# Channel norms of a two-block layer kernel: square roots and reciprocals taken once per token instead of on full tiles

## The reference, cut to what matters

```python
# first block, RWKV branch: the key's unit length over each head of 64 channels
kk = kk / jnp.maximum(jnp.sqrt(jnp.sum(kk * kk, axis=-1, keepdims=True)), 1e-12)
# after the scan: group norm over each head of 64 channels, then gain, bias, bonus, gate
mu = jnp.mean(y, axis=-1, keepdims=True)
var = jnp.mean(jnp.square(y - mu), axis=-1, keepdims=True)
y = (y - mu) * lax.rsqrt(var + GN_EPS) * gn_g + gn_b
y = (y + jnp.sum(r * k * r_k, axis=-1, keepdims=True) * v) * jax.nn.silu(gate)
# latents of both blocks: rmsnorm over 256, 128, 384 and 256 channels, layernorm over 64
y = xf * lax.rsqrt(jnp.mean(xf * xf, axis=-1, keepdims=True) + eps) * g
# second block, twice: rmsnorm over each head of 128 channels, times a gate
o = _rmsnorm(o, out_norm) * jax.nn.silu(g_raw)
```

## Time and profile before

| | us |
|---|---|
| median of 3 runs (6708.9 to 6734.62) | 6714.53 |
| the profiled execution, its own time | 6711.7 |
| its span | 6710.1 |

### The profile page before, as it was taken

One profiled execution on the slowest core, in us unless ns is written; L12 is line 12 of the kernel. 1 busy time (PEld: TensorE's weight loads), 2 busy tenths in 40 slices (PEclk: granted clock), 3 DMA queues, 4 the chain that ended last, 5 costly groups with the idle time before them and its releaser, 6 DMA issues. The chain is left out here.

```text
span 6710.1 us, 96643 instructions
## 1 busy us (share of the span) xinstructions
PE 5494.9 (82%) x37796; PEld 4606.1 (69%) x37797; DVE 3000.2 (45%) x4371; ACT 2172.1 (32%) x3224; POOL 263.6 (4%) x318
## 2 busy tenths in 40 slices
PE   5954774869685878999896859769999999999994
PEld 3642762657562457999785625659898898898994
DVE  3696334441264234555413633334444455554544
ACT  2212112532221334444422213223333344444432
POOL 0120000000010000000000100010000000000000
PEclk8976997979897888999898978879999999999997
DMA  2110001022000035555310000454444455555544
GB/s 72 39 44 2 3 13 57 1 109 72 16 0 28 7 123 226 204 206 201 139 63 13 0 32 2 167 177 159 156 160 155 163 184 189 184 188 188 188 160 167
DMA packets 112191, 714.18 MB, mean 106 GB/s; under 512 B 12960, under 2 KB 16816, under 8 KB 70320
## 3 DMA queue, kind: packets, MB, share of 16 engines
q1 hardware_dynamic: 96208, 657.53, 27.1%
q0 software_dynamic: 9184, 28.49, 1.2%
q10 hardware_dynamic: 6528, 24.12, 0.9%
HBM read 639.42 MB, written 70.67 MB: 106 GB/s over the span
## 5 line engine op out<-in xcount | busy, mean ns | idle before, releaser
L2702 DVE TENSOR_TENSOR experts_low<-experts_raw,experts_high 128x1024 fp32r<-128x1024 f32 x678 | 810.8, 1224 | 1000.5 <-ACT experts_high L2631 1000.5
L2566 PE MATMUL ps<-experts_xs_high,experts_high 128*128 128x256 f32 (+1 forms) x3584 | 1040.4, 290 | 31.6 <-issue 29.8
L2566 PE MATMUL ps<-experts_xs_low,experts_high 128*128 128x256 f32 (+1 forms) x3584 | 1040.0, 290 | 6.7 <-issue 6.7
L2566 PE MATMUL ps<-experts_xs_high,experts_low 128*128 128x256 f32 (+1 forms) x3584 | 1041.5, 291 | 0.0
L2566 PEld LDWEIGHTS ps<-experts_xs_high,experts_high 128*128 128x128 f32 x3584 | 682.3, 190 | 44.2 <-issue 34.7
L2631 ACT ACTIVATE experts_high<-experts_raw 128x1024 fp32r<-128x1024 f32 x678 | 687.7, 1049 | 63.1 <-DMA experts_raw<-experts 63.1
L2566 PEld LDWEIGHTS ps<-experts_xs_low,experts_high 128*128 128x128 f32 x3584 | 682.4, 190 | 16.3 <-issue 7.3
L2566 PEld LDWEIGHTS ps<-experts_xs_high,experts_low 128*128 128x128 f32 x3584 | 682.4, 190 | 0.0
L2250 PE MATMUL ps<-dense_xs_parts,dense_high 128*128 128x256 f32 x2816 | 499.2, 280 | 3.9 <-DVE dense_xs_parts L2353 2.7
L2250 PEld LDWEIGHTS ps<-dense_xs_parts,dense_high 128*128 128x128 f32 x2816 | 437.0, 189 | 12.2 <-issue 4.7
L2558 PE MATMUL ps<-experts_high,experts_hid_high 128*128 128x512 f32 x1120 | 445.1, 397 | 0.0
(11 more groups left out here) (492 smaller groups left out, 9428.1 us busy)
## 6 DMA issues: line engine op xcount, KB each, us to landing
experts_raw<-experts SPq DMA_DIRECT2D x226, 1536.0 KB, 6.4
dense_raw<-dense SPq DMA_DIRECT2D x90, 1536.0 KB, 6.6
proj_raw<-w_in SPq DMA_DIRECT2D x41, 512.0 KB, 3.6
y_slot<-route_blank SPq DMA_DIRECT2D x15, 1152.0 KB, 20.8
out_proj_raw<-w_out SPq DMA_DIRECT2D x48, 256.0 KB, 2.6
proj_keys_raw<-w_in SPq DMA_DIRECT2D x20, 512.0 KB, 3.5
x_mixed<-x_out SPq DMA_DIRECT2D x16, 512.0 KB, 4.8
y_slot<-experts_y ACTq DMA_DIRECT2D x8, 1024.0 KB, 8.7
```

What stands on the lines that cost most here:

```text
L2566: last = nc.tensor.matmul(ps[:, m, 0:width], w[:, u, m, c], x[:, k, 0:width], start=(k == 0 and i == 0), stop=(k == KD - 1 and i == 2))
L2702: nc.vector.tensor_tensor(low[:, v, t, :], raw[:, v % NR, t, :], high[:, v, t, :].bitcast(F32), ALU.subtract).then_inc(split, 1)
```

## The change

In all seven stages the sums are now formed with tokens on partitions. A block of 128 channels by 128 tokens of squares is PE's stationary operand, and one or two columns of ones move through it: out comes one number for each token (and head), with tokens on partitions. A tile gives 8 columns (16 with two heads to a tile). On this small array `stat` (`length` in `operands`, where all four tiles make one array of 64 columns) DVE scales, ACT takes the root, DVE inverts. Then ACT copies each number along 128 (64) columns into the tile that held the squares ("spread"), PE transposes the eight 128x128 blocks of it into PSUM ("turned"), and DVE multiplies it in from there. In `rwkv_out`, DVE's steps are also merged: gain and inverse in one instruction, bias and bonus in another. The tiles' steps are interleaved instead of step by step over all tiles, except in `operands`.

`head_norm_gate`, the core of it (`channel_norms` has the same form, with `ones` and groups of tiles):

```diff
@@ head_norm_gate, scalar
                 act.wait_ge(meansq, j + 1)
-                nc.scalar.activation(sq[:, j, :], sq[:, j, :], ACT.Sqrt).then_inc(rooted, 1)
+                nc.scalar.activation(stat[:, 1, j, :], stat[:, 0, j, :], ACT.Sqrt).then_inc(rooted, 1)
+                act.wait_ge(inverse, j + 1)
+                nc.scalar.activation(spread[j], stat[:, 2, j, :].unsqueeze(2).to_broadcast([P, NT, P]), ACT.Copy).then_inc(spreaded, 1)
@@ head_norm_gate, tensor
+            def sum_tokens(j):
+                pe.wait_ge(squared, j + 1)
+                if j >= 2:
+                    pe.wait_ge(meansq, j - 1)
+                for b in range(NT):
+                    last = nc.tensor.matmul(core.ps[:, 6 + j % 2, b:b + 1], sq[:, j, b * P:(b + 1) * P],
+                                            core.c("ones")[:, 0:1], start=True, stop=True)
+                last.then_inc(sums, 1)
+
+            def turn(j):
+                pe.wait_ge(spreaded, j + 1)
+                if j >= 3:
+                    pe.wait_ge(normed, j - 2)
+                for b in range(NT):
+                    last = nc.tensor.transpose(two(j)[:, b * P:(b + 1) * P], spread[j][:, b, :], core.c("eye"))
+                last.then_inc(turned, 1)
             for j in range(4):
-                pe.wait_ge(squared, j + 1)
-                for h in range(2):
-                    last = nc.tensor.matmul(core.ps[:, 2 * j + h, :], core.c("ones"), sq[:, j, h * HALF:(h + 1) * HALF],
-                                            start=True, stop=True)
-                last.then_inc(sums, 1)
+                sum_tokens(j)
+                if j >= 1:
+                    turn(j - 1)
+            turn(3)
@@ head_norm_gate, vector
+            def apply(j):
+                dve.wait_ge(gated, j + 1)
+                dve.wait_ge(turned, j + 1)
+                nc.vector.scalar_tensor_tensor(dst[:, j, :], dst[:, j, :], gain, two(j), ALU.mult, ALU.mult).then_inc(normed, 1)
...
```

`rwkv_operands`:

```diff
@@ scalar
+            act.wait_ge(lengths, 1)
+            nc.scalar.activation(length[:, 0, :], core.ps[:, 0, 0:8 * NT], ACT.Sqrt).then_inc(rooted, 1)
+            act.wait_ge(inverse, 1)
             for j in range(4):
-                act.wait_ge(heads, j + 1)
-                nc.scalar.activation(tmp[:, j, :], two(j), ACT.Sqrt).then_inc(rooted, 1)
+                nc.scalar.activation(tmp[:, j, :].rearrange("p (b n) -> p b n", b=2 * NT),
+                                     length[:, 2, 2 * NT * j:2 * NT * (j + 1)].unsqueeze(2).to_broadcast([P, 2 * NT, 64]),
+                                     ACT.Copy).then_inc(spreaded, 1)
@@ vector
+            nc.vector.tensor_scalar(length[:, 1, :], length[:, 0, :], 1e-12, None, ALU.max).then_inc(bounded, 1)
+            dve.wait_ge(bounded, 1)
+            nc.vector.reciprocal(length[:, 2, :], length[:, 1, :]).then_inc(inverse, 1)
             for j in steps:
...
-                dve.wait_ge(inverse, j + 1)
-                nc.vector.tensor_tensor(KK[:, j, :], KK[:, j, :], tmp[:, j, :], ALU.mult).then_inc(unit, 1)
+                dve.wait_ge(turned, j + 1)
+                nc.vector.tensor_tensor(KK[:, j, :], KK[:, j, :], two(j), ALU.mult).then_inc(unit, 1)
```

`rwkv_output`, DVE's new order:

```diff
+            def scale(j):
+                dve.wait_ge(centred, j + 1)
+                dve.wait_ge(turned, j + 1)
+                nc.vector.scalar_tensor_tensor(dev[:, j, :], dev[:, j, :], core.v("gn_g", j), two(1 + j % 3), ALU.mult, ALU.mult)\
...
+            for j in range(6):
+                if j < 4:
+                    invert(j)
+                if 1 <= j < 5:
+                    scale(j - 1)
+                if j >= 2:
+                    add(j - 2)
+                    give(j - 2)
```

More of the change, by code:

```diff
@@ L964, in _, with sum_tokens, turn @@
         def _(pe):
+            def sum_tokens(i):
+                g = groups[i]
+                pe.wait_ge(squared, sum(len(y[0]) for y in groups[:i + 1]))
+                if i >= 2:
+                    pe.wait_ge(meansq, i - 1)
+                for b in range(NT):
+                    for m, c in enumerate(g[0]):
+                        last = nc.tensor.matmul(core.ps[:, i % 2, b:b + 1], sq[:, c, b * P:(b + 1) * P],
+                                                core.c("ones")[:, 0:1], start=(m == 0), stop=(m == len(g[0]) - 1))
+                last.then_inc(sums, 1)
+            def turn(i):
+                pe.wait_ge(spreaded, i + 1)
+                for b in range(NT):
+                    last = nc.tensor.transpose(two(2 + 2 * i)[:, b * P:(b + 1) * P], spread[i][:, b, :], core.c("eye"))
+                last.then_inc(turned, 1)
             for i, g in centred:
@@ L968, in _ @@
                 last.then_inc(mean_ready, 1)
-            done = 0
-            for i, g in enumerate(groups):
-                done += len(g[0])
-                pe.wait_ge(squared, done)
-                for h in range(2):
-                    for m, b in enumerate(g[0]):
-                        last = nc.tensor.matmul(core.ps[:, 2 * i + h, :], core.c("heads" if g[4] else "ones"),
-                                                halves(sq[:, b, :], h), start=(m == 0), stop=(m == len(g[0]) - 1))
-                last.then_inc(sums, 1)
+            for i in range(len(groups)):
+                sum_tokens(i)
+                if i >= 1:
+                    turn(i - 1)
+            turn(len(groups) - 1)
         @block.scalar
@@ L1008, in _ @@
                     nc.vector.tensor_scalar(x[:, g[0][0], :], x[:, g[0][0], :], core.v(g[4], 0), None, ALU.add)
+            for i in range(len(groups)):
+                invert(i)
+                if i >= 1:
+                    apply(i - 1)
+            apply(len(groups) - 1)
     st.end()
@@ L1892, in head_norm_gate @@
     sq = st.sb("sq", [P, 4, T])
-    two = lambda j: core.ps[:, 2 * j:2 * j + 2, :].rearrange("p b n -> p (b n)")
-    squared, sums, gated, meansq, rooted, inverse = (st.sem(x) for x in ("squared", "sums", "gated", "meansq", "rooted", "inverse"))
+    stat = st.sb("stat", [P, 3, 4, NT])
+    spread = [sq[:, j, :].rearrange("p (b n) -> p b n", b=NT) for j in range(4)]
+    two = lambda j: core.ps[:, 2 * (j % 3):2 * (j % 3) + 2, :].rearrange("p b n -> p (b n)")
+    squared, sums, gated, meansq, rooted, inverse, spreaded, turned, normed = (
+        st.sem(x) for x in ("squared", "sums", "gated", "meansq", "rooted", "inverse", "spread", "turned", "normed"))
     with nc.Block(name) as block:
@@ L1913, in _, with turn @@
+            def turn(j):
+                pe.wait_ge(spreaded, j + 1)
+                if j >= 3:
+                    pe.wait_ge(normed, j - 2)
+                for b in range(NT):
+                    last = nc.tensor.transpose(two(j)[:, b * P:(b + 1) * P], spread[j][:, b, :], core.c("eye"))
+                last.then_inc(turned, 1)
+            for j in range(4):
+                sum_tokens(j)
+                if j >= 1:
+                    turn(j - 1)
+            turn(3)
         @block.vector
@@ L1915, in _ @@
             for j in range(4):
                 nc.vector.tensor_tensor(dst[:, j, :], dst[:, j, :], oT[:, j, :], ALU.mult).then_inc(gated, 1)
-                dve.wait_ge(sums, j + 1)
-                nc.vector.tensor_scalar(sq[:, j, :], two(j), 1.0 / P, 1e-6, ALU.mult, ALU.add).then_inc(meansq, 1)
-            def invert(j):
-                dve.wait_ge(rooted, j + 1)
-                nc.vector.reciprocal(sq[:, j, :], sq[:, j, :]).then_inc(inverse, 1)
-            invert(0)
-            for j in range(4):
-                if j < 3:
-                    invert(j + 1)
-                dve.wait_ge(gated, j + 1)
-                dve.wait_ge(inverse, j + 1)
-                nc.vector.scalar_tensor_tensor(dst[:, j, :], dst[:, j, :], gain, sq[:, j, :], ALU.mult, ALU.mult)
+                invert(j)
@@ L1930, in head_norm_gate @@
+                if j >= 1:
+                    apply(j - 1)
+            apply(3)
     st.end()
```

140 lines of the change are left out of this document (85 added, 55 removed).

## The result

The changed kernel takes **6596.6 us**, median of 4 runs (6594.8 to 6610.3), against 6711.7 for the kernel before beside it (4 runs, 6686.2 to 6734.6): a ratio of 0.9823, 95% interval 0.9802 to 0.9844. The forecast was 6601, range 6562 to 6622. The profiled execution's span is 6594.8 us at a mean clock of 0.902 (before 6710.1, 0.900). The total agrees, and so do most stages. A stage's length goes from its first PE or ACT row to its last DVE row, as in the prediction; `operands` goes from the first token sum to the first row of the step behind the norm.

What follows compares the result with a forecast made beforehand. The prediction took DVE, with its full-tile reciprocals, to bound the seven stages; their gains sum to 111.4 us, which from the profiled 6711.7 leaves 6600.3, stated as 6601 us, range 6562 to 6622.

Steps and rivals of the forecast that it cites:

- DVE itself sets the pace: All seven stages before the change: 23 full-tile reciprocals, 149.5 us in all, follow one another on DVE without idle waits.
- Pitch, clock and small steps: New steps' cost: 0.2133 us per sum record at clock 0.50, reciprocals 0.20 to 0.55 us, ACT's copy 1.06 us.
- The third rival: Token sums: weight loads can't run beside their matmuls, 0.695 us a record, net 120 us slower, 6831 us; chance 2%.
- `operands`, 18.6: Norm in `operands`: next step begins at 571.1 instead of 589.70, clock rising late in the turns; 18.6 us gained.
- `latent_norms`, 16.3: Stage `latent_norms`: starts warm out of the projections, ends at 128.5 instead of 144.87; 16.3 us gained.
- cold from 115 by the same choice: Sums of `latent_norms`: clock taken to fall at 115, an assumed time, as in `rwkv_out`, where no row shows it.
- bounds of 12.4 to 19.8: Gain of `latent_norms`: 12.4 us if the clock falls at once, 19.8 us if it never falls.
- `rwkv_out` (22.9: Stage `rwkv_out`: first sums warm, clock falling at 1023, DVE late at the end, 1046.4 against 1069.34; 22.9 us gained.
- Nothing else moves.: Outside the seven stages: same number of table loads, no DMA, later stages start from the same barrier; no change.
- The fourth rival: Whole kernel: something unseen, such as fetching longer instruction lists, refills the reciprocals' time; 6700 us or so, chance 3%.
- The first rival: Token sums: the clock goes up in them, terms sum to 151 us, total 6561 us; chance 17%.
- if PE waits in more places than for turn 3: Sign of being wrong; in `gated_norm` PE was to wait only for the last tile's transposes, some 0.3 us.

Runs made afterwards that it cites:

- e1_before: The kernel before, unchanged, run again to see whether its untouched loops repeat: ratio 0.9998 to the kernel before.
- e3_after: The changed kernel, unchanged, run a third time: 6607.0 us, ratio 0.9834 to the kernel before.
- e1_after: The changed kernel, unchanged, run once more: 6606.1 us, ratio 0.9824 to the kernel before.
- padded kernels: The kernel before with 76 or 38 small unread matmuls put ahead of PE's loop of chunks: 6732.6 us (1.0024) with 76, 6710.4 us with 38.
- e3_all128: The changed kernel with 128 columns moved for each token sum in all seven stages: 6567.9 us, ratio 0.9763 to the kernel before.

## Why the prediction was right, and where it was not

The mechanism and the price of the change were right. The close agreement of the total (6596.6 for 6601) is in part luck, as the fifth point says.

- **The bound.** "DVE itself sets the pace": shown. Without the reciprocals alone the stages lose what the reciprocals cost.
- **Pitch, clock and small steps.** 0.215 us a record at 0.50, reciprocals of 0.20 and 0.55, a copy of 1.05 in place of 1.06: as forecast. The third rival's 0.695 us a record is refuted by the same rows. `gated_norm` and `mla_norms`, 53.4 of the 109.5 us, rest on these alone, and each term was within 0.1. (`mla_norms1` was that close with the profile it was taken from; `e1_before` has 35.3 there, not 33.8.)
- **`operands`, 18.6 for 19.1.** The clock rose in the turns, as the prediction read from L1025, only sooner: 32 turns took 5.04 us, not 6.84. In `e3_after` it rose later, they took 6.62, and the norm 23.8 us.
- **`latent_norms`, 16.3 for 14.6.** The mis-sized term. "cold from 115 by the same choice" was a choice with no row, 3.9 us after the first sum. The clock fell 2.4 us after it, and the stage took 1.7 us longer; in `e1_after`, cold from before its first sum, the gain was 13.5 (38.0 - 24.5), inside the bounds of 12.4 to 19.8. In `rwkv_out` (22.9 for 22.5) the same choice was nearer: 3.9 us taken, 2.9 measured.
- **"Nothing else moves."** Wrong. The span fell by 115.3 us, 109.5 in the stages and 5.8 elsewhere, and those 5.8 are a balance: chunks 26.9 shorter, against 4.5 us more in the projection of the keys, 4.0 and 14.0 more in the two gated stages, and 1.4 less in the rest. The 26.9 and the 14.0 repeat in the later profiles. The 4.5 and 4.0 don't: `e1_after` has 310.6 us in the projection against 312.1 in `e1_before`, and before's first gated loop varies by 6.6. The padded kernels show that the place of PE's code alone gives the 26.9; that it gives the 14.0 is likely, as the second loop got longer with both pads, but its clock's cause is open. The total was hit partly by that balance: without the gated stages' 18 us it would have lain some 22 under the forecast. The fourth rival named fetching as a cost; it works in both directions. (From 6714.5, the median, the prediction's own gain leads to 6603, not 6601: 2.8 us were left out of that step.)
- **The first rival.** Refuted for this kernel: no clock above 0.50 in the sums of `gated_norm` and `mla_norms`. But its price was right, as `e3_all128` shows.
- **PE's waits.** "if PE waits in more places than for turn 3": once started, it waits nowhere in `gated_norm`; turn 3's 0.3 us was covered. In `rwkv_out` it waits twice, 1.26 us ahead of turn 0, behind the table load that the prediction counted, and 0.60 ahead of turn 3.

## What to carry to other kernels

A reciprocal of a value that is the same along a row or a head belongs on the small operand, even if PE has to turn it back. Where PE takes over work in matmuls of few columns, read the granted clock under them, and try the same matmul with 128 columns when banks allow: its record cost nothing more here and brought 39 us. Compare changes by stage and not by total when loops elsewhere shift: here code in front of a loop moved that loop by 27 us.

## What the runs showed of the hardware

- The granted clock stayed at 0.50 under 80 gapless records of one column (17.2 us) and 64 of 64 columns (13.9 us), and reached 1.00 under 128-column ones. In `latent_norms` a clock that was up stayed up under 64 columns (1.00, 114 to 117) and fell under one (0.50 from 114.1).
- Under turns by PE, 128x128 float32, in `operands`, the clock went from 0.50 to 1.00, 2.7 us after their start in one profile and 6.0 in another.
- ACT's copy with a stride-0 operand costs the price of the full tile, 1.05 us for 128x1024.
- PE's waits at a loop's jump, 2.2 to 3.7 us each, came 12, 6 or 3 times in six iterations for 0, 38 and 76 matmuls put ahead of the loop, each with a packet of the instruction queue. An iteration without a packet had no wait.
